# Output projections: the first gate summed at the end of the first chunk, the last norm between feeds, copies behind the block loads

## The reference

```
h, gate = ada_modulate(x, cond, w_ada, b_ada, norm_g)   # rms_norm(x) * (1 + scale) + shift
z = h @ w_in
...
y_b = gqa_attend(qr, k_all, v_all) * silu(g_b)                 # layer 0, beside y_a, a gated MLP
out = concatenate([y_a, y_b]) @ w_out
...
o = rms_norm(diff_attend(qr, k_all, v_all, lam), sub_g) * (1 - LAMBDA_INIT_1)   # layer 1, per head
out = (o * silu(g)) @ w_out
...
x = x + gate * out
```

## Time and profile before

| | us |
|---|---|
| median of 3 runs | 2814.64 (2814.32 to 2815.84) |
| profiled execution | 2815.88 |
| span of the profiled execution | 2814.3 |
| TensorE busy | 2564.7 (91%) |
| VectorE busy | 1723.1 (61%) |
| ScalarE busy | 809.5 (29%) |
| GpSimd busy | 426.2 (15%) |
| mean granted TensorE clock | 0.965 |

### The profile page before, as it was taken

How to read it: one execution, slowest core, us unless ns; L and a number is a source line. 1 busy time by engine, 2 the same in 40 slices (tenths; PEclk the granted TensorE clock), 3 DMA queues, 4 the chain that set the end, 5 groups by cost and what they waited for, 6 DMA issues and landing times.

```text
span 2814.3 us, 38162 instructions
## 1 busy us (share of the span) xinstructions
PE 2564.7 (91%) x12040; PEld 2016.7 (72%) x12040; DVE 1723.1 (61%) x3165; ACT 809.5 (29%) x1698; POOL 426.2 (15%) x481
## 2 busy tenths in 40 slices
PE   6999999998898799979999999998999999977995
PEld 1258877777777678868877777777777777756884
DVE  1335788887787447766355656655666565554675
ACT  2012232232222222222233333333333333322221
POOL 0000222220222100000122222222221211011001
PEclk8999999999999899989999999999999999988998
DMA  7745544444444455644322222222232322245555
GB/s 269 248 148 163 195 141 153 136 145 158 156 159 148 155 186 192 221 154 144 119 92 89 88 85 84 85 92 85 68 101 86 98 91 87 83 136 203 184 193 201
DMA packets 165601, 395.42 MB, mean 141 GB/s; under 512 B 15008, under 2 KB 15648, under 8 KB 160992
## 3 DMA queue, kind: packets, MB, share of 16 engines
q1 hardware_dynamic: 132304, 249.08, 28.0%
q0 software_dynamic: 33168, 144.72, 14.6%
HBM read 332.93 MB, written 63.18 MB: 141 GB/s over the span
## 4 chain that ended last, share of the span: by engine, by line
PE 60%; DVE 18%; DVEq 7%; issue 6%; ACT 4%; DMA 3%; POOL 0%; ACTq 0%; SPq 0%; POOLq 0%
PE ps L554 46%; DVE w_lo L1142 4%; PE ps L440 3%; PE ps L583 3%; PE ps L449 3%; DVE small L1030 3%; PE ps L458 2%; DVEq L1165 2%; DVE work L1047 2%; ACT w_hi L773 1%; DMA w_raw<-in_w_ada_dram 1%; DVE wT_lo L1022 1%; PE ps L541 1%; DVEq L1052 1%; DVEq L1028 1%
## 5 line engine op out<-in xcount | busy, mean ns | idle before, releaser
L554 PE MATMUL ps<-w_hi,hT_hi 128*128 128x512 f32 x2800 | 1148.3, 410 | 15.6 <-DVE stage L1159 8.1
L554 PE MATMUL ps<-w_hi,hT_lo 128*128 128x512 f32 x2800 | 1108.6, 396 | 0.0
L554 PE MATMUL ps<-w_lo,hT_hi 128*128 128x512 f32 x2800 | 1103.1, 394 | 0.0
L1142 DVE TENSOR_TENSOR w_lo<-w_raw,w_hi 128x512 fp32r<-128x512 f32 x560 | 406.1, 726 | 355.4 <-ACT w_hi L773 337.6
L554 PEld LDWEIGHTS ps<-w_hi,hT_lo 128*128 128x128 f32 x2800 | 532.3, 190 | 119.5
L554 PEld LDWEIGHTS ps<-w_hi,hT_hi 128*128 128x128 f32 x2800 | 535.4, 191 | 112.4 <-issue 13.2
L554 PEld LDWEIGHTS ps<-w_lo,hT_hi 128*128 128x128 f32 x2800 | 535.4, 191 | 92.1 <-issue 1.4
L773 ACT CAST w_hi<-w_raw 128x512 fp32r<-128x512 f32 x560 | 346.6, 621 | 482.4 <-PE ps L554 464.0
L1172 DVE SCALAR_TENSOR_TENSOR ada_sum<-w_raw,cond,ada_sum 128x512 f32<-128x512 f32 x480 | 366.7, 805 | 34.7 <-issue 10.1
L724 ACT ACTIVATE work<-ps,small 128x640 f32<-128x640 f32 (+1 forms) x200 | 141.9, 710 | 595.9 <-DVE small L1033 595.9
L440 PE MATMUL ps<-consts,work 128*128 128x128 f32 x768 | 134.9, 290 | 68.7 <-DVE q_low_lo L1022 19.7
(11 more groups left out here) (185 smaller groups left out, 2427.6 us busy)
## 6 DMA issues: line engine op xcount, KB each, us to landing
w_raw<-in_w_in_dram SPq DMA_DIRECT2D x216, 512.0 KB, 3.9
w_raw<-in_w_ada_dram SPq DMA_DIRECT2D x256, 256.0 KB, 3.0
z<-stage POOLq DMA_DIRECT2D x27, 1280.0 KB, 5.1
w_raw<-in_w_ada_dram SPq DMA_DIRECT2D x64, 512.0 KB, 4.7
w_raw<-in_w_out_dram SPq DMA_DIRECT2D x64, 512.0 KB, 4.2
work<-z POOLq DMA_DIRECT2D x72, 320.0 KB, 3.7
work<-o POOLq DMA_DIRECT2D x8, 1280.0 KB, 8.1
x<-stage POOLq DMA_DIRECT2D x7, 1280.0 KB, 11.7
```

What stands on the lines that cost most here:

```text
L554: last = nc.tensor.matmul(ps[:, t, :], x[:, kt, t * P:(t + 1) * P], w[:, kt % RING, :], start=(kt == 0 and i == 0), stop=(kt == KT - 1 and ...
L1142: nc.vector.tensor_tensor(w_lo[:, kt % RING, :], w_raw[:, w_at(c, kt), kt % 2, :], w_hi[:, kt % RING, :].bitcast(F32), ALU.subtract).then_ ...
```

## The change

In both layers, the sum of chunk 0's gate moves from ahead of the chunk to its slot 76 (k tile 15, second token tile), and TensorE no longer waits in front of the chunk for it. On VectorE `ada_gate` moves from ahead of the feeds to the end of chunk 0, in front of the multiplies, and the wait for `o_free` with it. The last head's norm in layer 1 is taken in threes after each of the three first feed steps. On GpSimd, the head's store and the wait for its landing move behind the loads of block 1, the wait for the stage's store goes between load y and load g of block 1, and the tables, copies and the drain move behind the last block's loads and the load of the old x. No arithmetic is changed; a drain of VectorE ahead of the first chunk's multiplies is gone.

```diff
--- before.py
+++ after.py
@@ -674,9 +674,7 @@
 
             pe.wait_ge(sp_free, 10)
             pe.wait_ge(S[0].t_free, 8 * L0.n_bank + 1)
-            sum_finish(8, True)
-            pe.wait_ge(mod_free, 10)
-            project_chunk(C_O0, 11, F=1)
+            project_chunk(C_O0, 11, finish_at(76, 8, True), F=1)
             with pe.Fori(1, 4) as j:
                 project_chunk(j + C_O0, j + 11, finish_at(72, j + 8, True))
 
@@ -694,9 +692,7 @@
                 finish(steps)
 
             pe.wait_ge(S[1].t_free, 16 * L1.n_bank + 1)
-            sum_finish(12, True)
-            pe.wait_ge(mod_free, 14)
-            project_chunk(C_O1, 31, F=3)
+            project_chunk(C_O1, 31, finish_at(76, 12, True), F=3)
             with pe.Fori(1, 4) as j:
                 project_chunk(j + C_O1, j + 31, finish_at(72, j + 12, True))
 
@@ -1392,14 +1388,15 @@
 
             def output(first, F, n0, m0, last):
 
-                if F == 3:
-                    finish(norm_out(dve))
+                last_norm = norm_out(dve) if F == 3 else iter(())
+                for k in range(FEED):
+                    feed_step(F, k)
+                    for _ in range(3):
+                        next(last_norm, None)
+                finish(last_norm)
+                split_chunk(first, feed_beside(F))
                 dve.wait_ge(S[F // 2].o_free, (8 if F == 1 else 16) + 1)
                 ada_gate(m0, n0)
-                for k in range(FEED):
-                    feed_step(F, k)
-                split_chunk(first, feed_beside(F))
-                dve.drain()
                 for t in range(TT):
                     multiply(first, t)
 
@@ -1654,10 +1651,7 @@
             load_y(0, 0)
             wait(S[0].t_ready, 80)
             load_g(0, 0)
-            store_head(L0, 7)
-            free_head(L0, 7)
             store_stage(10, z_at(0, 10))
-            free_stage(10)
 
             def feed_y(l, F):
 
@@ -1666,21 +1660,45 @@
                     if b >= 2:
                         wait(turn_ready, 16 * F + 4 * (b - 1))
                     load_y(l, b)
+                    if b == 1:
+                        wait(stage_stored, (10 if l == 0 else 30) * 16 + 16)
                     load_g(l, b)
+                    if b == 1:
+                        store_head(L1 if l else L0, 15 if l else 7)
+                        free_head(L1 if l else L0, 15 if l else 7)
                 wait(turn_ready, 16 * F + 12)
 
-
-            wait(kn_stored, 16 * 8)
-            for t, n in ((rope_c, 0), (rope_s, 1)):
-                pool.dma_start(t[:, :], a["rope"][1, n]).then_inc(copied, 16)
-            for g in range(2):
-                pool.dma_start(new_k0[0][:, g, :], kn_d[4 * g]).then_inc(copied, 16)
-            pool.dma_start(new_v0[0].rearrange("t h d -> t (h d)"), z_d[0][0, :, TS, 256:512]).then_inc(copied, 16)
+            def results0():
+
+                wait(kn_stored, 16 * 8)
+                for t, n in ((rope_c, 0), (rope_s, 1)):
+                    pool.dma_start(t[:, :], a["rope"][1, n]).then_inc(copied, 16)
+                for g in range(2):
+                    pool.dma_start(new_k0[0][:, g, :], kn_d[4 * g]).then_inc(copied, 16)
+                pool.dma_start(new_v0[0].rearrange("t h d -> t (h d)"), z_d[0][0, :, TS, 256:512]).then_inc(copied, 16)
+
+            def results1():
+
+                for g in range(4):
+                    heads = slice(4 * g, 4 * g + 4)
+                    pool.dma_start(new_k1[0][:, heads].rearrange("t h m d -> t (h m d)"),
+                                   z_d[1][3 * g + 1, :, TS, :]).then_inc(copied, 16)
+                    pool.dma_start(new_v1[0][:, heads].rearrange("t h d -> t (h d)"),
+                                   z_d[1][3 * g + 2, :, TS, :]).then_inc(copied, 16)
+                pool.drain()
+                for j in range(4):
+                    pool.dma_start(last_g[j], a["final_g"][j * NC:(j + 1) * NC].unsqueeze(0).to_broadcast([P, NC])).then_inc(
+                        fg_in, 16)
 
             def output(l, F, n0, s0, src, dst):
 
                 feed_y(l, F)
                 load_old(src, 0)
+                free_stage(10 if l == 0 else 30)
+                if l == 0:
+                    results0()
+                else:
+                    results1()
                 wait(gb_free, n0 + 1)
                 load_bias(l, 1)
                 dst = dst.rearrange("t p d -> p t d")
@@ -1764,19 +1782,6 @@
             wait(S[1].t_ready, 160)
             load_g(1, 0)
             store_stage(30, z_at(1, 15))
-            store_head(L1, 15)
-            free_head(L1, 15)
-            free_stage(30)
-            for g in range(4):
-                heads = slice(4 * g, 4 * g + 4)
-                pool.dma_start(new_k1[0][:, heads].rearrange("t h m d -> t (h m d)"),
-                               z_d[1][3 * g + 1, :, TS, :]).then_inc(copied, 16)
-                pool.dma_start(new_v1[0][:, heads].rearrange("t h d -> t (h d)"),
-                               z_d[1][3 * g + 2, :, TS, :]).then_inc(copied, 16)
-            pool.drain()
-            for j in range(4):
-                pool.dma_start(last_g[j], a["final_g"][j * NC:(j + 1) * NC].unsqueeze(0).to_broadcast([P, NC])).then_inc(
-                    fg_in, 16)
             output(1, 3, 4, 31, x1, x2_d)
 
             for j in range(4):
```

## The result

| | before | changed |
|---|---|---|
| median | 2815.24 us (4 runs, 2814.32 to 2816.4) | 2789.25 us (4 runs, 2779.65 to 2791.5) |
| profiled execution | 2815.88 | 2779.65 |
| span | 2814.3 | 2778.1 |
| interval of layer 0 (below) | 146.44 | 141.26 |
| interval of layer 1 (below) | 159.95 | 139.36 |

The ratio is 0.9904, 95% interval 0.9881 to 0.9927. The forecast was 2789.4.

What follows compares the result with a forecast made beforehand. Projection matmuls fill nearly half the span, so only TensorE's idle or low-clock time can be won. Layer 0 -4.9 and layer 1 -20.3, together -25.2, turn 2815.88 into 2790.7; 1.24 lower for the median, 2789.4 us, range 2785.5 to 2793.

Steps and rivals of the forecast that it cites:

- Part 1: Gate leaves the start: feed block 0 3.2 us earlier in layer 0, first transposes 12.4 us earlier in layer 1.
- Part 3: GpSimd's queue: block 1's loads directly follow block 0's feed; fifth transposes 5.9 us (layer 0) and 20.8 us (layer 1) earlier.
- Part 2: Layer 1's last head's norm between feeds: pieces overrun VectorE's free time, +1.8 us, bounds 0 and 6.8.
- rival (a): Block 1's loads bind, the stage's store being in their way: +11 us, 2800.4 us; chance 0.16.
- this cover: Layer 1: block 1's load g lands at 2526.8, ahead of VectorE coming to feed it at 2527.1; 0.3 us.
- clock terms: Step behind the fifth transposes, without the hole's clock loss: -1.4 us in layer 0, -1.9 in layer 1.
- Part 4: Gate's sum inside chunk 0 costs +1.72 us per layer, TensorE's wait for the first multiply +0.65 per layer.
- (b): Low clock isn't entered in layer 1's start; four transpose groups save 2.5 us: 2786.9 us; chance 0.10.
- (c): Low clock stays on past the chunk's start: 6.4 k tiles eat the gain, eight give 2821 us; chance 0.03.
- (d): The feeds are not what is waited for; the time stays at 2814.6 us; chance 0.03.

Runs made afterwards that it cites:

- e1: The changed kernel again, no edit: median 2788.50 us, ratio 0.9906, intervals 141.49 (layer 0) and 140.17 (layer 1).
- e3: Against the kernel before, only gate, sum and norm moved, GpSimd's queue untouched: median 2828.35 us, ratio 1.0041.
- e2: Against the kernel before, only GpSimd's tables, copies and drain moved behind the last block's loads: median 2802.08 us, ratio 0.9939.
- e4: Against the changed kernel, layer 1's last head's norm taken whole in front of feed block 0: median 2793.93 us, layer 1 interval 145.26.
- e5: Against the changed kernel, the last head's store and its landing wait put in front of block 1's loads: median 2804.69 us.
- e6: Against the changed kernel, unused filler matmuls added while TensorE waits in the starts: median 2793.72 us, intervals 141.84 and 138.92.

## Why the prediction was right

**Part 1** held to 0.4 us. Counted from the start of the gated eviction, feed block 0 was to begin after 6.75 us in layer 0 and 3.76 in layer 1; it began after 6.62 and 3.77, and in e1 after 7.12 and 3.77. In layer 0 what ended last was block 0's load, as written; VectorE's timeline of the changed kernel:

```profile
959.02 2.83 DVE L1246 SCALAR_TENSOR_TENSOR work<-work 128x2560 f32<-128x2560 f32 x1 [2.89 <-DMA work<-z]
```

What the prediction did not say is what this part is worth without Part 3. I gave the parts as steps of one sum, which was safe, since each fifth transposes' time was worked out with both in place. The e3 run shows what a reader who prices the edits one by one would have got wrong: the move of the gate and the norm alone costs 11.7 us.

**Part 2** was forecast at 1.8 and measured 1.52: 10.40 us between the first and the fourth transposes against three steps of 2.96.

**Part 3**: the fifth transposes came 6.06 (layer 0) and 21.11 us earlier (5.80 and 20.18 in e1), for 5.9 and 20.8. Behind the last projection matmul of the chunk before they came 22.9 and 20.9 us, for 22.8 and 20.8. The load of block 1 was covered in both layers, so rival (a) fell. In layer 1 it had more room than forecast: load g landed 8.2 us after its issue, at 2509.3, not the 10.7 that I took, and VectorE came 2.4 us later (2.1 in e1), where I had sized this cover at 0.3. The 10.7 had been measured behind four table loads. In layer 1 this load took 10.7 and 11.1 us where the tables stood in front of it (before, e3), 9.4, 9.7 and 9.3 without them (e2, e4, e5), and 8.2 and 8.5 in the changed kernel (first profile, e1), where moreover load y had gone out 2.2 us ahead of it, not 0.9. In layer 0 the cover was small, 0.6 us for 0.8 (9.7 us of load), as e6 showed: with the feed 1.8 us faster the load ended last by 1.58.

One step of the working did not agree with itself: with the 5.4 us that layer 0 was given for the first k tile, layer 1's fifth transposes would have started at 2530.6, 23.9 after the eviction began, and not at 2530.0. The first profile has 22.9 there and e1, whose first k tile ran at the low clock for longer, 23.8. In the first profile VectorE's feed block 1 ended last (at 2514.53), in e1 TensorE's k tile.

The step behind the fifth transposes took 3.98 and 4.05 us, for 3.97: the clock terms of 1.4 and 1.8 came.

**Part 4**: the sum and the wait for the multiply were forecast at 2.37. What is left of the intervals, when the fifth transposes and the step behind them are taken off, is 2.29 and 2.33. The wait of TensorE itself was 0.38, not 0.65: the gate started 1.92 us after the sum and took 1.51, not 2.02 and 1.59, so the first multiply ended 4.11 us after the sum's start, not 4.35, while TensorE's three slots ended at 3.80 as forecast. The sum itself, 1.72 forecast, and what else lies in the chunk make up the other 1.9; I can't split them. The drain of VectorE that the change leaves out was not tested by itself.

**Rivals (b) and (c).** The clock fell in layer 1 too, just as the transposes began (busy time by stretch, columns as in the earlier trace rows; 0.62 is the mean granted clock of the first microsecond, 0.55 that of the second):

```profile
2498.00:2499.00 1.00, 0.52 (x3) 0.55 (x4) 0.31 (x1) 0.00 (x0) 0.06 (x1) 0.62 1.15 471
...
2511.00:2512.00 1.00, 1.00 (x4) 0.81 (x3) 1.00 (x2) 0.46 (x1) 0.28 (x1) 0.55 0.16 53
```

and it came up within the first k tile, here at about 2511.9, in both profiles of the changed kernel. The forecast left it open how fast; that is the 0.93 us between the changed kernel's two layer 1 profiles at the fifth transposes. Rival (c), the only slower one, did not occur, and (d) fell with the total. The drain of GpSimd took 12.99 us in its new place instead of 7.96, and it didn't matter: the last table load was issued by 2565.68, 9 us before the gate.

**The total.** 2789.4 was the median of before less 25.2. The intervals give 25.8, and the medians 26.0, but in the runs of e1 the medians give 28.0. The profiled execution, for which the sum gives 2790.7, took 2779.65. So the mechanism and the two intervals are what was forecast well; that the median meets it to 0.2 us is luck, as the end of the document shows. The range of the forecast itself (2785.5 to 2793) does not come out of the terms that it names: with Part 2 and the wait of Part 4 at nothing the sum is 2786.3.

## What to carry to other kernels

A stage's start can be held by two queues in series: an early first block was worth less than nothing here, because the second block's load still stood behind the same things (e3), and a small store in front of that load took back most of the gain (e5). So follow the issuing queue to the second and the third block before an edit is priced. Ask of every wait whether it is for the data or for the buffer: here the gate was cheap, and the wait in front of it was for the place where its result was to go. And measure a change of 1% in an interval of the trace that holds nothing else, since the total may scatter by as much as half of it.

## What the runs showed of the hardware

The total also moves with TensorE's waits and clock in places that the change doesn't touch. In the changed kernel's first profile the gated eviction of layer 0 began at 952.40, in the one before at 960.95, 8.55 us later, after the same instructions. Some 4 us of this lie in one chunk. Its first matmul, and the busy time by stretch just behind it, in the kernel before and then in the changed one (in the second row the granted clock is the last number but two):

```profile
718.13 0.71 PE L554 MATMUL ps<-w_hi,hT_hi 128*128 128x512 f32 x1 [2.67 <-DVE stage L1159]
720.00:730.00 10.00, 8.75 (x43) 7.49 (x42) 2.83 (x6) 1.91 (x5) 2.04 (x3) 0.75 0.54 204
```

```profile
712.63 0.50 PE L554 MATMUL ps<-w_hi,hT_hi 128*128 128x512 f32 x1 [1.63 <-DVE stage L1155]
720.00:730.00 10.00, 9.99 (x50) 8.18 (x49) 7.72 (x15) 3.74 (x9) 3.79 (x5) 1.00 0.77 272
```

In the kernel before, TensorE had waited 2.67 us for VectorE's eviction, and the clock fell as the matmuls began again; in the changed kernel it had waited 1.63 us (1.64 in e1), and the clock stayed at the high level. The longer wait is 1.0 of the 4 us, the rest came behind it. Why VectorE was later there in one execution is open.

The four runs of the changed kernel fit: spans of 2778.1, 2786.6, 2788.7 and 2789.9 us at mean clocks of 0.971, 0.969, 0.967 and 0.965. By these means the time at the low level grows from 161 to 195 us. Were TensorE the bound throughout, half of the 34 us would be lost, 17; the spans differ by 11.8. That is an inference from rows, and no experiment kept TensorE busy in those places. It isn't the whole of the scatter either: two runs of e1, both at 0.969, have spans of 2781.9 and 2788.9 us. The kernel before scattered as much once it was run more often: 16 runs of it taken beside e1 lay between 2810.67 and 2822.88, where the first three had lain within 1.5 us. In e6 the filler raised the mean clock to 0.972 to 0.974 and made neither the total nor layer 0 faster: there the load ended last, and a high clock is worth something only where TensorE is what ends last.
